# RWKV recurrence: 16x16 diagonal inverses by row substitution on VectorE instead of three doubling levels on TensorE

## The reference, cut to what matters

```python
def step(s, inp):
    w_t, k_t, v_t, kk_t, b_t = inp[:5]
    sk = jnp.einsum('dbhvk,dbhk->dbhv', s, kk_t)
    s = s * w_t[..., None, :] - sk[..., None] * b_t[..., None, :] + v_t[..., None] * k_t[..., None, :]
    y = jnp.einsum('dbhvk,dbhk->dbhv', s, inp[5]) if len(inp) == 6 else None
    return s, y
```

## Time and profile before

| | |
|---|---|
| median of three runs | 3546.51 us (3545.18 to 3549.38) |
| the profiled execution, its span | 3543.43 us, 3541.6 us |
| TensorE busy in the span | 3325.1 us, 94% |
| VectorE, ScalarE, GpSimd | 1563.3 us, 1293.9 us, 1097.7 us |
| recurrence of layer 0, of layer 1 | 250 to 948 us, 2210 to 2800 us |

### The profile page before, as it was taken

How to read it: one execution, slowest core, us unless ns; L and a number is a source line. 1 busy time by engine, 2 the same in 40 slices (tenths; PEclk the granted TensorE clock), 3 DMA queues, 4 the chain that set the end, 5 groups by cost and what they waited for, 6 DMA issues and landing times. The chain is left out here.

```text
span 3541.6 us, 82858 instructions
## 1 busy us (share of the span) xinstructions
PE 3325.1 (94%) x36717; PEld 2675.4 (76%) x36717; DVE 1563.3 (44%) x2511; ACT 1293.9 (37%) x2253; POOL 1097.7 (31%) x695
## 2 busy tenths in 40 slices
PE   6999999999988999999999899999999998899998
PEld 4668888888765777887878676787777766678887
DVE  4243334443287646412121734444544386471324
ACT  3333233333265424422212243334333375343322
POOL 2111132232111533332333232114333213445543
PEclk8999999999999999999999999999999999999999
DMA  7754332442221443233332146344443323423332
GB/s 275 246 178 117 112 108 87 129 132 80 86 78 65 137 165 96 90 119 119 119 119 84 53 138 190 99 110 125 132 120 90 108 81 122 165 87 113 95 96 89
DMA packets 444286, 420.81 MB, mean 119 GB/s; under 512 B 15588, under 2 KB 371082, under 8 KB 437018
## 3 DMA queue, kind: packets, MB, share of 16 engines
q1 hardware_dynamic: 442346, 406.73, 36.6%
q10 hardware_dynamic: 1584, 8.78, 0.6%
HBM read 326.72 MB, written 88.74 MB: 117 GB/s over the span
## 5 line engine op out<-in xcount | busy, mean ns | idle before, releaser
L917 PE MATMUL ps<-I-321_h_hi,I-324_w_hi 128*128 128x512 f32 (+1 forms) x1376 | 507.1, 369 | 13.0 <-PEq L126 13.0
L917 PE MATMUL ps<-I-322_h_lo,I-324_w_hi 128*128 128x512 f32 (+1 forms) x1376 | 482.6, 351 | 0.5 <-issue 0.5
L917 PE MATMUL ps<-I-321_h_hi,I-325_w_lo 128*128 128x512 f32 (+1 forms) x1376 | 481.7, 350 | 0.0
L375 PE MATMUL ps<-I-321_h_hi,I-324_w_hi 128*128 128x512 f32 (+1 forms) x1448 | 429.5, 357 | 6.0 <-PEq L126 2.4
L2583 POOL TENSOR_TENSOR I-325_w_lo<-I-323_w_raw,I-324_w_hi 128x1024 fp32r<-128x1024 f32 x116 | 279.0, 2406 | 498.8 <-ACT I-324_w_hi L2546 498.8
L375 PE MATMUL ps<-I-321_h_hi,I-325_w_lo 128*128 128x512 f32 (+1 forms) x1448 | 423.8, 353 | 0.0
L375 PE MATMUL ps<-I-322_h_lo,I-324_w_hi 128*128 128x512 f32 (+1 forms) x1448 | 420.9, 351 | 0.0
L881 POOL TENSOR_TENSOR I-325_w_lo<-I-323_w_raw,I-324_w_hi 128x1024 fp32r<-128x1024 f32 x68 | 166.5, 2448 | 590.7 <-ACT I-324_w_hi L1161 590.7
L2546 ACT ACTIVATE I-324_w_hi<-I-323_w_raw 128x1024 fp32r<-128x1024 f32 x118 | 125.1, 1060 | 524.6 <-PE ps L375 332.0
L917 PEld LDWEIGHTS ps<-I-321_h_hi,I-324_w_hi 128*128 128x128 f32 x1376 | 261.8, 190 | 53.7 <-issue 13.6
L375 PEld LDWEIGHTS ps<-I-321_h_hi,I-324_w_hi 128*128 128x128 f32 x1448 | 234.9, 188 | 88.4 <-issue 46.5
(11 more groups left out here) (913 smaller groups left out, 7015.7 us busy)
## 6 DMA issues: line engine op xcount, KB each, us to landing
I-323_w_raw<-in_w_in SPq DMA_DIRECT2D x134, 512.0 KB, 5.7
I-323_w_raw<-in_ffn_up SPq DMA_DIRECT2D x88, 512.0 KB, 3.8
I-19239_ada_w<-in_ada_w SPq DMA_DIRECT2D x24, 1024.0 KB, 6.0
I-323_w_raw<-in_ffn_down SPq DMA_DIRECT2D x44, 512.0 KB, 3.3
proj_d<-I-2019_result SPq DMA_DIRECT2D x52, 384.0 KB, 2.9
I-513_ada_w<-in_ada_w SPq DMA_DIRECT2D x16, 1024.0 KB, 5.6
I-330_gate<-proj_d SPq DMA_DIRECT2D x24, 384.0 KB, 3.2
proj_d<-I-25096_result SPq DMA_DIRECT2D x36, 256.0 KB, 2.6
```

The source lines that it names most:

```text
L375: m = pe.matmul(dst[:, at:at + n], w[wi][:, k, :], a[ai][:, k, at:at + n], start=k == 0 and i == 0, stop=k == kt - 1 and i == 2)
L917: m = pe.matmul(bank(6 + i % 2, n_c), w[:, k, :], hv[:, k, c0:c0 + n_c], start=k == 0 and v == 0, stop=k == KT - 1 and v == 2)
```

## The change

The inverses of the 16x16 diagonal blocks are made by substitution, row by row, on VectorE, for both directions and all 64 blocks a partition group at once; levels 0 to 2 fall away and levels 3 and 4 stay (FIRST = 3, N_LV = 2). The products that started T and TT fall away with their masks. VectorE takes NAT's diagonal blocks (mask `own`), packs them by a reduction into `coef`, and in step k fetches row k of the growing inverse into all 16 partitions of its block with `stream_shuffle`, multiplies by column k and adds. The result goes into Y; a 32x32 block transpose makes T, and ScalarE copies Y into TT with partition halves swapped where `row_of` wants them (`swapped`). The scalings are cut in two: `scaled` keeps Kt, Bh and EN; `scaled_rest` (Bp, Lr, rk, R) of direction 1 runs ahead of that direction's masks in its own group, all else of the next group's scalings behind levels 3 and 4. Five of the fills move to "turn1", the place behind the last transposes.

```diff
-            points = ["prod0", "turn0", "prod1", "turn1"] + [f"{k}{n}" for n in range(5) for k in ("Y", "offT")]
+            points = ["prod0", "turn0", "prod1", "turn1"] + [f"{k}{n}" for n in range(N_LV) for k in ("Y", "offT")]
             points += ["W1", "W2", "U0", "S0", "U1", "S1", "end"]
-            wanted = ["prod0", "prod1", "W1", "W2", "U0", "S0", "U1", "S1"] + [f"Y{n}" for n in range(5)] + [f"offT{n}" for n in range(5)]
-            wanted += ["end", "turn1", "turn0"] + [f"offT{n}" for n in range(5)] + ["W1", "prod0", "prod1"]
+            wanted = ["prod0", "prod1", *("turn1",) * 5, "W1", "W2", "U0", "S0", "U1", "S1"] + [f"{k}{n}" for k in ("Y", "offT") for n in range(N_LV)]
+            wanted += ["end", "turn0", "turn1"] + [f"offT{n}" for n in range(N_LV)] + ["W1", "prod0", "prod1", "W2"]
...
                             product(0, 0, Bh[d], Kt[d], True)
-                            product(0, 256, Kt[d], Bh[d], True)
                             product(2, 0, EN[d], Kt[d])
...
-                            product(4, 256, Bh[d], Kt[d])
                             fill(f"prod{d}", g)
...
+                        n_far = len(FAR) * C
+                        for d in range(2):
+                            act.wait_ge(sem(f"base{d}"), g + 1)
+                            for i in range(2):
+                                act.activation(TT[d][rows(i), 0:n_far], Y[d][rows(1 - i), 0:n_far], ACT.Copy)
+                            act.activation(TT[d][:, n_far:GCOL], Y[d][:, n_far:GCOL], ACT.Copy).then_inc(sem(f"swapped{d}"), 1)
...
+                            if g and d:
+                                scaled_rest(g, 1)
+                            dve.wait_ge(sem("pmm"), n_p + 1)
                             dve.tensor_tensor(o4(NAT[d][:, :]), pv(0, 0), mk(strict), ALU.mult).then_inc(sem("prod"), 1)
-                            dve.tensor_tensor(o4(T[d][:, :]), pv(0, 256), mk(lo1), ALU.mult).then_inc(sem("prod"), 1)
...
+                        for d in range(2):
+                            dve.tensor_copy(inv[:, d], bc(masks[:, M_BASE, (1 + d) * BASE:(2 + d) * BASE], 8))
+                            dve.wait_ge(sem("prod"), before(n_pr, g, d) + 1)
+                            dve.tensor_tensor(by_block(T[d][:, :]), by_block(NAT[d][:, :]), own, ALU.mult).then_inc(sem("sub"), 1)
+                        for d in range(2):
+                            dve.wait_ge(sem("sub"), n_s + 2)
+                            dve.tensor_reduce(coef[:, d, :, flip(d)], by_block(T[d][:, :]).rearrange("p m b c -> p m c b"),
+                                              mybir.AxisListType.X, ALU.add).then_inc(sem("sub"), 1)
+                        dve.wait_ge(sem("sub"), n_s + 4)
+                        dve.tensor_tensor(inv[:, :, :, 0:1], inv[:, :, :, 0:1], coef[:, :, :, 0:1], ALU.add).then_inc(sem("sub"), 1)
+                        for k in range(1, BASE - 1):
+                            n_k = n_s + 5 + 4 * (k - 1)
+                            dve.wait_ge(sem("sub"), n_k)
+                            for d in range(2):
+                                k_row = BASE - 1 - k if d == 0 else k
+                                dve.stream_shuffle(row_k[:, d, :, 0:k + 1], inv[:, d, :, 0:k + 1],
+                                                   [i // BASE * BASE + k_row for i in range(32)]).then_inc(sem("sub"), 1)
+                            dve.wait_ge(sem("sub"), n_k + 2)
+                            dve.tensor_tensor(term[:, :, :, 0:k + 1], row_k[:, :, :, 0:k + 1],
+                                              coef[:, :, :, k:k + 1].to_broadcast([P, 2, 8, k + 1]), ALU.mult).then_inc(sem("sub"), 1)
+                            dve.wait_ge(sem("sub"), n_k + 3)
+                            dve.tensor_tensor(inv[:, :, :, 0:k + 1], inv[:, :, :, 0:k + 1], term[:, :, :, 0:k + 1],
+                                              ALU.add).then_inc(sem("sub"), 1)
+                        dve.wait_ge(sem("sub"), n_s + 4 * BASE - 3)
+                        for d in range(2):
+                            dve.tensor_tensor(by_block(Y[d][:, :]), bc(inv[:, d, :, flip(d)], C // BASE, 2), own, ALU.mult).then_inc(sem(f"base{d}"), 1)
+                        for d in range(2):
+                            dve.wait_ge(sem(f"base{d}"), g + 1)
+                            dve.transpose(T[d][:, :], Y[d][:, :]).then_inc(sem(f"T{d}"), 1)
+                        for v in range(N_LV):
+                            n_lv = FIRST + v
...
                             if g + 1 < N_G:
-                                if n_lv == 2:
+                                if v == 0:
                                     sums(g + 1, 0)
-                                elif n_lv == 3:
+                                if v == 1:
                                     scaled(g + 1, 0)
-                                elif n_lv == 4:
+                                    scaled_rest(g + 1, 0)
+                                if v == N_LV - 1:
                                     sums(g + 1, 1)
```

More of the change, by code:

```diff
@@ L67 @@
 LEVELS = (1, 2, 4, 8, 16, 32)
-(M_ID, M_LO, M_UP, M_LOI, M_UPI, M_LO1, M_UP1) = range(7)
+BASE = 16
+FIRST = 3
+N_LV = 2
+(M_LO, M_UP, M_LOI, M_UPI, M_BASE) = range(5)
 def tables():
@@ L82, in tables @@
     low = lambda b: (row // b == col // b + 1) & (row // b % 2 == 1)
-    m = [row == col, row > col, row < col, row >= col, row <= col, low(1), low(1).T]
+    base = np.zeros((C, C), bool)
+    base[:, 0:C // BASE] = row[:, 0:C // BASE] // BASE == col[:, 0:C // BASE]
+    base[:, BASE:2 * BASE] = row[:, 0:BASE] % BASE == BASE - 1 - col[:, 0:BASE]
+    base[:, 2 * BASE:3 * BASE] = row[:, 0:BASE] % BASE == col[:, 0:BASE]
+    m = [row > col, row < col, row >= col, row <= col, base]
     t["masks"] = np.ascontiguousarray(np.concatenate([np.stack(m, 1)] * 2, 0).astype(np.float32))
-    lv = [low(b) for b in LEVELS[1:]] + [low(b).T for b in LEVELS[1:]]
+    lv = [low(b) for b in LEVELS[FIRST + 1:]] + [low(b).T for b in LEVELS[FIRST + 1:]]
     t["lvmasks"] = np.ascontiguousarray(np.concatenate([np.stack(lv, 1)] * 2, 0).astype(np.int32))
@@ L696, in rwkv_scan @@
             two = lambda name: [sb(s2, f"{name}{d}", G) for d in range(2)]
-            masks = sb(s2, "masks", [P, 7, C])
-            lvm = sb(s2, "lvmasks", [P, 10, C], I32)
+            masks = sb(s2, "masks", [P, 5, C])
+            lvm = sb(s2, "lvmasks", [P, 2 * N_LV, C], I32)
+            coef, inv = (sb(s2, n, [P, 2, 8, BASE]) for n in ("coef", "inv"))
             reset = sb(s2, "reset", [P, GCOL])
@@ L707, in rwkv_scan @@
             MV, U, W2s = Y, T, NAT
+            row_k, term = (T[d][:, 0:16 * BASE].rearrange("p (d m c) -> p d m c", d=2, m=8) for d in range(2))
             sg, Lr, EN, a, Bh, Bp = (two(n) for n in ("sg", "Lr", "EN", "a", "Bh", "Bp"))
@@ L731, in rwkv_scan @@
             n_fm = [6 if w else 5 for w in want]
-            n_pr = [6 if w else 4 for w in want]
+            n_pr = [4 if w else 2 for w in want]
             before = lambda n, g, d: 2 * sum(n[:g]) + d * n[g]
@@ L992, in across @@
                             beside = [(across_one, n_lv, hh, t) for hh, t in NEAR]
-                            beside += [(flipped_one, n_lv - 1, 1, t) for t in range(CTILES)] if n_lv else []
+                            beside += [(flipped_one, n_lv - 1, 1, t) for t in range(CTILES)] if n_lv > FIRST else []
                             for n, (hh, t) in enumerate(FAR):
@@ L1033, in _ @@
                                     m.then_inc(sem(f"offT{d}"), 1)
-                            fill(f"offT{n_lv}", g)
+                            fill(f"offT{v}", g)
                         for d in range(2):
@@ L1278, in _ @@
                         scaled(0, d)
+                        scaled_rest(0, d)
                     dve.wait_ge(sem("const"), 32)
@@ L1305, in _ @@
-                            dve.tensor_tensor(g8(TT[d][:, :]), g8(TT[d][:, :]), m8(M_ID), ALU.add).then_inc(sem(f"T{d}"), 1)
-                        for n_lv in range(5):
-                            if n_lv:
+                        n_s = (4 * BASE - 3) * g
+                        by_block = lambda ap: ap.rearrange("p (m b c) -> p m b c", b=C // BASE, c=BASE)
+                        flip = lambda d: slice(None, None, -1) if d == 0 else slice(None)
+                        own = bc(bc(masks[:, M_BASE, 0:C // BASE], BASE, 2), 8)
@@ new lines, in _ @@
+                        dve.wait_ge(sem("sub"), n_s + 4 * BASE - 3)
[4 more added lines that the diff above has]
+                            dve.transpose(T[d][:, :], Y[d][:, :]).then_inc(sem(f"T{d}"), 1)
+                        for v in range(N_LV):
+                            n_lv = FIRST + v
+                            if v:
```

70 lines of the change are left out of this document (34 added, 36 removed).

## The result

The change makes the kernel 1.1% faster: 3507.2 us (median of 4 runs, 3505.2 to 3511.5) against 3547.8 us for the kernel before on the same chip, a ratio of 0.9888 with a 95% interval of 0.9871 to 0.9905. The prediction was 3573 us, slower. The time lies in its range and on the other side of no change. The profiled execution has a span of 3506.8 us, 34.8 less than before.

What follows compares the result with a forecast made beforehand. Time was taken as TensorE's own work plus its gaps, VectorE counting only where TensorE waits. -164 + 144 + 26 + 15 + 5 = +26 us on 3543.4 gave 3569.5, as a median 3573 us, range 3450 to 3640.

Steps and rivals of the forecast that it cites:

- T of the first direction ready at 35.8 us: Time from TensorE's first product of the second direction to T, summed as 3.5 + 20.1 + 2.2 + 10 us.
- gaps: TensorE idle ahead of the first level left, waiting for T: 58 us in layer 0, 86 in layer 1, +144 us.
- Ahead of the steps: VectorE through with the output masks at 3.5 us, then copies, multiplications, reductions and an addition: 3.3 us.
- Steps and shuffles: Fourteen substitution steps on VectorE: 14.9 us with shuffles priced as copies, plus 2.2 us a group, between 0 and 4.3.
- GpSimd's loss: VectorE's two-SBUF-input operations wait while GpSimd runs: 2.2 us per split, 3.2 per rotation, 10 us a group.
- The cover: TensorE's products, parts and transposes while VectorE makes T: mean 26.2 us in layer 0, 21.0 in layer 1.
- stops inside the products: TensorE's stops late in the row of products, 28 us over both layers; layer 0's 17 us taken as gained.
- slow clock: After each of twelve gaps TensorE's granted clock is low, 2.2 us of work lost or a little more: +26 us.
- W1T: TensorE waits for VectorE's copy of W1T behind the next group's scalings and sums, five groups of layer 1: +15 us.
- The last of the prediction's "wrong if": TensorE would wait for weights because ScalarE and GpSimd can't split them at the pace of six parts in a row.
- the one in which short operations slip between GpSimd's: VectorE's chain loses nothing to GpSimd, T ready at 25.8 us: 3430 us; chance 0.29, wholly or in half.
- its half version: Half of GpSimd's delay to VectorE's chain stays: about 3500 us; shares the chance of 0.29 with the whole.

Runs made afterwards that it cites:

- g1_shuffles: The changed kernel with every shuffle of the 14 steps issued twice, the first time into columns nobody reads: 3560.0 us, ratio 1.0034 to the kernel before.
- e4_turn7: The changed kernel with only the list of the parts' places changed, seven behind the second direction's transposes and none behind the first's: 3480.0 us.
- f2_psum7: The changed kernel with the steps' coefficients and products in PSUM, seven parts at "turn1", and the second direction's sums and scaled_rest moved later: 3385.4 us.

## Why the prediction was wrong

The step that failed is the one that has T of the first direction ready at 35.8 us, which set the gaps at +144 us. In the mean of the 12 groups the prediction had 35.6 us; the trace has 32.2. Term by term, from the rows of all groups:

- Ahead of the steps: 3.5 + 3.3 = 6.8 us forecast, 7.3 where nothing interferes (5.8 in the two groups without an output), 8.2 in the mean. The reductions took 1.05 us each, not 0.69.
- Steps and shuffles: 14.9 + 2.2 forecast, 15.3 measured. The shuffle lies near the lower bound: 0.19 us for 16 elements, 0.29 for 120, which is the price of a multiplication of the same size within 0.03 us, and its mask costs 0.01. The estimate from the Trainium skill (VectorE: DVE Perf Modes, "The perf-mode tier table"), 0.11 us more per shuffle than a tensor_tensor and 3.0 us a group, is not borne out at these sizes: the steps with their shuffles took 0.4 us more than the 14.9.
- GpSimd: 10 forecast, 6.8 in the steps and 1.1 ahead of them (part of the 8.2). The price was near (two splits in a chain cost 3.8 us, 1.9 each for 2.2; a rotation 2.8 for 3.2), the number was not: 26 splits and 13 rotations met the steps, where 32 and 16 were counted from the order of the slots.
- Behind: 1.9 forecast, 1.95 measured.

So two terms were too large, GpSimd's loss and the shuffle's, and the reductions took back some of it.

The cover was 27.6 us in layer 0 for 26.2 (waits among the parts lengthen it) and 21.0 in layer 1, as forecast. Gaps: 26 us for 58, and 71.5 for 86. g1_shuffles adds 4.0 us, 0.6 more than was missing, which makes up for the longer cover of layer 0; it has the forecast's 144 us, and is slower than the kernel before. So the mechanism and the slope (12 us per us; 11.7 in gaps, 13 with the clock) were right, and the size was 3.4 us in 35.6 too large. The prediction had the sign turn at about 33.5 us, the runs at 35.3: with T alone as forecast the time would have been about 3552 us, no faster than the kernel before, and the rest of the error lies in the other terms.

The other terms, forecast and measured (us, both layers):

```
levels                           -110   -112   190.5 less 78.8, the two that stay at full clock
two products                      -23    -28
stops inside the products         -17    -28   all of them
wait ahead of the first level      -5     -5
between the state updates          -9    -11   9.4 of waits, 2 of slow clock
other waits of before               0    -10
gaps                             +144    +98
slow clock                        +26    +28   parts +16, matmuls right behind the gaps +12
W1T                               +15    +10
scaled_rest ahead of products      +5     +2
ScalarE's shifted copies            0    +19   not foreseen
sum                               +26    -37   the stretches: -36.6
```

The gaps make 46 of the 63 us of error. The stops make 11: the prediction left layer 1's in, and the changed kernel has none in either layer. That is no law for rows of four products (e4_turn7 has 7.1 us of them, f2_psum7 4.1): they are waits for TensorE's instructions, which the prediction didn't look for. The last of the prediction's "wrong if" came true in part: a late ScalarE held up TensorE, though by its shifted copies and not by the weights. Of the rivals, the one in which short operations slip between GpSimd's did not happen in its mechanism, 1.9 us of each split being lost; its half version, 3500, lies near the result for other reasons.

## What to carry to other kernels

When a change trades one large sum for another, here 164 us against 190, each a product of a small difference and a count, the sign is that of the difference: work out the turning point (33.5 us forecast, about 35.3 by the runs) and give the chances by how surely the chain lies on either side of it. A chain of short two-operand operations on VectorE beside a busy GpSimd loses its waits when one operand is put into PSUM: 64 us here. When a chain is just too long for its cover, compare shortening it, taking contention from it and moving cover to it: 86, 64 and 27 us here, and 122 with the second and third together and two moves of order. A stop that the list of waits doesn't explain can be the engine waiting for its own instructions: here 28.1 us of stops in long rows of small matmuls, each of which ended just behind a packet of the instruction queue.

## What the runs showed of the hardware

A shuffle took 0.19 us for 16 to 32 elements in each partition, 0.22 for 40 to 64, 0.26 for 72 to 96 and 0.29 for 104 to 120: it went up in steps of 32 elements. A copy of 128 elements within SBUF took 0.22 us. The shuffles lost next to nothing to GpSimd (under 0.2 us a group, 28 of them together). VectorE's operations with one operand in SBUF and one in PSUM did not wait for GpSimd's splits at all, at sizes from 32 to 240 elements, and took no longer than with both in SBUF (0.41 us for 240 elements in either place). A reduction of 512 elements to 128 with strided input took 1.05 us where an elementwise operation on 512 took 0.69. TensorE's instructions came in packets of 16 KB, some 252 matmuls and weight loads each. Rows of 96 small matmuls (192 records and as many weight loads) stopped for 0.5 to 3.4 us, rows of 64 stopped not at all in the changed kernel and up to four times in others (0.3 to 2.4 us), and each stop ended 1.1 to 1.6 us after such a packet had landed. Behind ten of the eleven gaps of the changed kernel (4.9 to 15.7 us) TensorE was granted 0.50 to 0.55, and 64 small matmuls took 2.5 to 2.7 us instead of 1.52; behind the one of 2.2 us it kept 1.00.
